# Gate rows of the mLSTM layer: three transfers inside SBUF and two VectorE additions in place of two selecting matmuls

## The chip, the cores and the metric

One core of one Trainium2 chip runs the whole program. The metric is device time in microseconds. TensorE (PE) does the matmuls, VectorE (DVE), ScalarE (ACT) and GpSimd (POOL) work beside it, SyncE (SP) issues most transfers; SBUF is the on-chip memory of 128 partitions, PSUM the matmuls' result memory of 8 banks.

## The reference, cut to what matters

The program is a trunk of two layers over 512 tokens of width 1024: layer 0 mixes tokens by an mLSTM, layer 1 by differential attention; both add a cross-attention into 256 memory tokens and a SwiGLU. The change touches the two gates of the mLSTM, eight columns of the first projection:

```python
h = rmsnorm(x, norm1[0])
p = h @ w_in
gates = p[..., 4 * MIX_WIDTH:4 * MIX_WIDTH + 2 * M_HEADS] + gate_b
i_pre, f_pre = gates[..., :M_HEADS], gates[..., M_HEADS:]
...
log_f = jax.nn.log_sigmoid(f_pre)
bc = jnp.cumsum(log_f, axis=-1)
```

Beside it stands the memory's projection, `rmsnorm(mem, mem_norm) @ w_mem_kv`, whose first tile comes right behind the changed place on PE.

## The kernel before, in words

Activations lie transposed: partitions are features, the free axis holds the 512 tokens. Every float32 product is made of three matmuls on rounded parts: a weight tile of 128 columns is split into `w_hi` (its rounding) and `w_lo` (the rest), an activation into `Hh`/`Hl` (or `Ah`/`Al`), and PE adds hi·hi, hi·lo and lo·hi over 8 chunks: 24 matmuls for a tile. POOL makes `w_hi` of a tile with one instruction (L561) and `w_lo` with four (L566); for tile n of the first projection it waits until PE is done with tile n-3 (`dense_done`), whose slot it overwrites. SP loads the raw weights ahead.

The order of the work is written out by hand in one list per engine; semaphores join them. The first projection's tiles are `PROJ`: q0, q1, v0, v1, m0, q2, m1, q3, m2, q4, m3, v2, ... (q for query and key columns, v for values, m for the memory's keys and values, 256 tokens wide). Each result leaves its PSUM bank through VectorE (`scaled_out`, `mem_out`), which divides by the norm and frees the bank.

How the gates are computed before the change:
- In the first tile, PE also multiplies by `wg`, whose columns 0 to 7 are the rounded gate weights and 8 to 15 their rests. Bank 6 then holds 16 rows: input gate, forget gate (4 heads each) by the rounded weights, and the same two groups of 4 by the rests.
- VectorE scales these 16 rows into `tmp[6]` (L1113) and raises `g_free`.
- The first half of a gate's value plus its second half is wanted on partitions 0 to 3. PE does both at once with two fp32 matmuls by the 0/1 matrix `C_GSEL` (L1628, L1629): the input gate goes to bank 6, the forget gate to bank 3. Semaphore `gsel_done`.
- ScalarE (L688 to L693) takes the forget gate from bank 3 through bias, Abs, Exp and Ln; VectorE (L1143 to L1149) forms the running sums; L1147 reads the input gate from bank 6.

The places beside it that the prediction speaks of: `mem_lo(0)` on VectorE (L1048, called after L1127) makes the low part `Al` of the memory's eight chunks with eight instructions that read `mT` and `Ah`, both in SBUF; `m_tile(0)` on PE is tile m0 and waits chunk by chunk for them (`mg_ready`); ahead of it stands the small matmul on `rm` (`mss_done`), and behind it `v_tr(0)`, four transposes. `first_tap(c)` is ScalarE's first step of the convolution, `conv(c)` VectorE's other three; `lamw` and `lame` (L1126, L1127) are two tiny VectorE instructions of the second layer's lambda. `link(...)` makes an engine wait for its own instruction before it issues the next. `dense_free` counts freed banks. `b_sq` (L876) is the second layer's place where ScalarE issues transfers inside SBUF (`QKR<-QKP`, 32 rows each), and L511 SP's transfer of the 4 rows of `Mrow` to a DRAM tensor, on which the next transfers of that queue (L515) wait.

```python
v_tile(1)
pe.wait_ge(g_free, 1)
pe.wait_ge(std_done, 1)
mm(PS[0:MH, 6], cn[0:16, C_GSEL:C_GSEL + MH], tmp[6][0:16, 0:SEQ])
mm(PS[0:MH, 3], cn[0:16, C_GSEL + MH:C_GSEL + 2 * MH], tmp[6][0:16, 0:SEQ]).then_inc(gsel_done, 1)
pe.wait_ge(msum_done, 1)
mm(PS[:, 7, 0:MEM], ones[:], rm[:]).then_inc(mss_done, 1)
m_tile(0)
v_tr(0)
q_tile(2)
```

Of the kernel before, what the change touches and what calls it, by code (L numbers as in the profile page):

```python
# [28 lines left out]
ALU = mybir.AluOpType  # L29
ACT = mybir.ActivationFunctionType  # L30
# [4 lines left out]
SEQ = 512  # L35
# [7 lines left out]
MH = 4  # L43
# [22 lines left out]
C_ID, C_BD, C_ROT, C_NEG, C_BIG, C_SEL, C_GSEL, C_INV = 0, 128, 256, 384, 512, 640, 640 + MH * P, 640 + MH * P + 8  # L66
# [52 lines left out]
def at_tile(kind, i):  # L119
    return PROJ.index((kind, i))  # L120
# [46 lines left out]
def hybrid_trunk(nc, x_t, mem_t, positions, wt, wg_cols, a_gate_b, b_lambda, prm_cols, con, out):  # L167
    ctx = ExitStack()
    with ctx:
        def sb(name, shape, dt=F32, scope=ctx):  # L170
            return scope.enter_context(nc.sbuf_tensor(name, shape, dt))

        def sem(name):
            return ctx.enter_context(nc.semaphore(name))

        PS = ctx.enter_context(nc.psum_tensor("PS", [P, 8, 512], F32))
# [10 lines left out]
        cn = sb("cn", [P, N_CON])  # L187
# [23 lines left out]
        tmp = [sb(f"tmp{i}", [P, 516]) for i in range(8)]  # L211
# [13 lines left out]
        gb = sb("gb", [MH, 2], scope=sA)  # L225
# [49 lines left out]
        g_free = sem("g_free")  # L275
# [37 lines left out]
        gsel_done = sem("gsel_done")  # L313
# [267 lines left out]
        def _(act):  # L581
            link_n = [0]

            def link(ins):
                link_n[0] += 1
                ins.then_inc(ach, 1)
                act.wait_ge(ach, link_n[0])
# [42 lines left out]
            def mem_hi(l):  # L630
                for k in range(KD):
                    nc.scalar.activation(flat(Ah[:, 4 * l:4 * l + 4])[:, k * MEM:(k + 1) * MEM],
                                         mT[:, k], ACT.Copy,
                                         scale=gcol[:, R_MN + 8 * l + k:R_MN + 8 * l + k + 1]).then_inc(mhi, 1)

            def first_tap(c):
                act.wait_ge(dense_free, at_tile("q", c) + 1)
                if c == 1:
                    act.wait_ge(mstd_done, 1)
                if c >= 2:  # L640
                    act.wait_ge(qk_ready, c - 1)
                nc.scalar.activation(PS[:, CV_BANK[c % 2]], tmp[2 + c % 2][:, 3:3 + SEQ], ACT.Identity,
                                     scale=gcol[:, R_CW + 3 * QKC + c:R_CW + 3 * QKC + c + 1],
                                     bias=gcol[:, R_CB + c:R_CB + c + 1]).then_inc(conv_first, 1)
# [34 lines left out]
            nc.scalar.activation(msq.rearrange("p n k -> p k n"), mT[:], ACT.Square).then_inc(msq_done, 1)  # L679
            mem_hi(0)  # L680
            first_tap(0)
            act.wait_ge(mss_done, 1)
            nc.scalar.activation(rm[:], PS[:, 7, 0:MEM], ACT.Sqrt, scale=1.0 / D, bias=epsc[:]).then_inc(mstd_done, 1)
            first_tap(1)
            v_out(0)

            act.wait_ge(gsel_done, 1)
            link(nc.scalar.activation(tmp[0][0:MH, 0:SEQ], PS[0:MH, 3], ACT.Identity, bias=gb[:, 1:2]))  # L688
            link(nc.scalar.activation(tmp[1][0:MH, 0:SEQ], tmp[0][0:MH, 0:SEQ], ACT.Abs))
            link(nc.scalar.activation(tmp[1][0:MH, 0:SEQ], tmp[1][0:MH, 0:SEQ], ACT.Exp, scale=-1.0))  # L690
            act.wait_ge(lam_s, 1)
# [319 lines left out]
        def _(dve):  # L1011
            link_n = [0]

            def link(ins):
                link_n[0] += 1
                ins.then_inc(vch, 1)
                dve.wait_ge(vch, link_n[0])

            def col(r):
                return gcol[:, r:r + 1]  # L1020
# [102 lines left out]
            link(nc.vector.tensor_scalar(gx[:, 4:5], col(R_BK), 8.0, None, ALU.mult))  # L1123
            nc.vector.tensor_copy(gx[:, 3:4], col(R_BQ)).then_inc(gx_ready, 1)
            dve.wait_ge(lam_in, 32)
            link(nc.vector.tensor_tensor(lamw[:], lamv[0:1, 0:4:2], lamv[0:1, 1:4:2], ALU.mult))  # L1126
            nc.vector.tensor_reduce(lame[0:1, 0:2], lamw[:], AX.X, ALU.add).then_inc(lam_s, 1)  # L1127
            mem_lo(0)
# [9 lines left out]
            b_row, a_row = tmp[5][0:MH, 0:SEQ], tmp[6][0:MH, 0:SEQ]  # L1138
# [2 lines left out]
                                           ALU.add, ALU.subtract).then_inc(lam_d, 1)  # L1141
            dve.wait_ge(lnf_done, 1)
            link(nc.vector.scalar_tensor_tensor(L, F, 0.0, L, ALU.min, ALU.subtract))  # L1143
            link(nc.vector.memset(tmp[7][0:MH, 0:SEQ], 1.0))
            dve.wait_ge(vT_done, 2)
            link(nc.vector.tensor_tensor_scan(b_row, tmp[7][0:MH, 0:SEQ], L, 0.0, ALU.mult, ALU.add))
            link(nc.vector.scalar_tensor_tensor(a_row, PS[0:MH, 6], gb[:, 0:1], b_row, ALU.add, ALU.subtract))  # L1147
            link(nc.vector.tensor_tensor_scan(Mrow[:], a_row, a_row, 0.0, ALU.max, ALU.max))
            nc.vector.tensor_tensor(tmp[0][0:MH, 0:SEQ], Mrow[:], b_row, ALU.add).then_inc(a_ready, 1)  # L1149
            mem_out(1)  # L1150
# [373 lines left out]
        def _(pe):  # L1524
            def mm(out_, a, b, start=True, stop=True):
                return nc.tensor.matmul(out_, a, b, start=start, stop=stop)  # L1526
# [98 lines left out]
            v_tile(1)  # L1625
            pe.wait_ge(g_free, 1)
            pe.wait_ge(std_done, 1)
            mm(PS[0:MH, 6], cn[0:16, C_GSEL:C_GSEL + MH], tmp[6][0:16, 0:SEQ])  # L1628
            mm(PS[0:MH, 3], cn[0:16, C_GSEL + MH:C_GSEL + 2 * MH], tmp[6][0:16, 0:SEQ]).then_inc(gsel_done, 1)  # L1629
            pe.wait_ge(msum_done, 1)  # L1630
            mm(PS[:, 7, 0:MEM], ones[:], rm[:]).then_inc(mss_done, 1)
            m_tile(0)
# [518 lines left out]
```

## Time and profile before

| what | value |
|---|---|
| median of 3 runs | 1240.56 us (1239.69 to 1241.76) |
| the profiled execution | 1240.49 us, its span 1238.7 us |
| PE busy | 1231.1 us, 99% |
| POOL busy | 840.9 us, 68% |
| DVE busy | 512.7 us, 41% |
| ACT busy | 352.1 us, 28% |
| instructions | 15969 |

Times in the rows are microseconds from the start of the span unless marked ns. A row of a timeline gives the start, the duration, engine, line, operation, result and sources, how many were merged, and in brackets how long the engine was idle before it and what ended that. An issue of a transfer has a q behind its engine's name. The time beyond the span lies around the profiled instructions.

### The profile page before, as it was taken

What the parts mean: (1) busy time and instruction counts of PE and PEld (TensorE: products, weight loads), DVE (VectorE), ACT (ScalarE), POOL (GpSimd) and SP (SyncE); (2) the same over time, 40 slices, a digit from 0 to 9 for tenths busy, and PEclk for the clock granted to TensorE, in tenths of its full rate; (3) what the DMA queues carried; (4) which work ended last, traced back from release to release, by engine and by line L of the source; (5) the groups of instructions that cost most, each with busy time, mean ns of one, the idle gap of its engine ahead of it and who ended that gap; (6) DMA issues with size and microseconds to landing.
All of it is one profiled execution on the core that took longest, in us unless ns stands there. A gap on an engine that the chain in (4) does not pass through costs nothing.

```text
span 1238.7 us, 15969 instructions
## 1 busy us (share of the span) xinstructions
PE 1231.1 (99%) x5800; PEld 1000.1 (81%) x5800; DVE 512.7 (41%) x787; ACT 352.1 (28%) x700; POOL 840.9 (68%) x1029
## 2 busy tenths in 40 slices
PE   9999999999999999999999999999999999999998
PEld 7888877788888888888887777778888888888887
DVE  6954434634322233112344777775433112221331
ACT  6523456543210011001141666645322001100110
POOL 7998333467777777777776444436687777777775
PEclk9999999999999999999999999999999999999999
DMA  7234111122332222222233222222222223222223
GB/s 271 92 120 153 68 52 40 64 86 94 102 102 89 98 102 87 100 102 98 76 132 102 70 69 69 62 77 67 89 97 101 94 94 102 97 90 102 94 73 105
DMA packets 35067, 116.99 MB, mean 94 GB/s; under 512 B 4417, under 2 KB 4930, under 8 KB 34886
## 3 DMA queue, kind: packets, MB, share of 16 engines
q1 hardware_dynamic: 33416, 112.82, 26.8%
q10 hardware_dynamic: 1598, 3.51, 1.1%
q8 instruction: 29, 0.48, 0.2%
q14 instruction: 24, 0.20, 0.1%
HBM read 111.05 MB, written 2.11 MB: 91 GB/s over the span
## 4 chain that ended last, share of the span: by engine, by line
PE 94%; DVE 2%; POOL 1%; ACT 1%; DMA 1%; SPq 0%; issue 0%; DVEq 0%; POOLq 0%; ACTq 0%
PE PS L1526 92%; DMA w_raw<-in_wt_dram 1%; POOL w_lo L566 1%; PE PS L1920 0%; DVE nmB L1432 0%; DVE PS L1031 0%; SPq L475 0%; DVE Al L1256 0%; DVE PB L1444 0%; PE PS L1765 0%; PE PS L1948 0%; DVE PB L1443 0%; PE PS L1891 0%; DVE PS L1430 0%; PE PS L1883 0%
## 5 line engine op out<-in xcount | busy, mean ns | idle before, releaser
L566 POOL TENSOR_TENSOR w_lo<-w_raw,w_hi 128x256 fp32r<-128x256 f32 (+1 forms) x800 | 613.6, 797 | 17.0
L561 POOL TENSOR_SCALAR w_hi<-w_raw 128x1024 fp32r<-128x1024 f32 (+2 forms) x204 | 214.4, 1051 | 365.3 <-PE PS L1526 365.1
L1526 PE MATMUL PS<-Hh,w_hi 128*128 128x512 f32 x1072 | 428.6, 400 | 1.0 <-POOL w_lo L550 0.6
L1526 PE MATMUL PS<-Hh,w_lo 128*128 128x512 f32 x1072 | 418.1, 390 | 0.0
L1526 PE MATMUL PS<-Hl,w_hi 128*128 128x512 f32 x1072 | 418.1, 390 | 0.0
L1526 PEld LDWEIGHTS PS<-Hh,w_hi 128*128 128x128 f32 x1072 | 201.4, 188 | 54.2 <-issue 12.9
L1526 PEld LDWEIGHTS PS<-Hh,w_lo 128*128 128x128 f32 x1072 | 201.3, 188 | 43.0
L1526 PEld LDWEIGHTS PS<-Hl,w_hi 128*128 128x128 f32 x1072 | 201.6, 188 | 39.5 <-issue 1.0
L1526 PE MATMUL PS<-Ah,w_hi 128*128 128x512 f32 (+1 forms) x544 | 208.0, 382 | 0.1
L1526 PE MATMUL PS<-Ah,w_lo 128*128 128x512 f32 (+1 forms) x544 | 205.1, 377 | 0.0
L1526 PE MATMUL PS<-Al,w_hi 128*128 128x512 f32 (+1 forms) x544 | 205.0, 377 | 0.0
L1526 PEld LDWEIGHTS PS<-Ah,w_hi 128*128 128x128 f32 x544 | 102.4, 188 | 21.9 <-issue 2.1
L1526 PEld LDWEIGHTS PS<-Ah,w_lo 128*128 128x128 f32 x544 | 102.3, 188 | 19.0
L852 ACT ACTIVATE tmp<-tmp 128x512 f32<-128x512 f32 x44 | 27.9, 635 | 315.1 <-DVE tmp L1356 315.1
L1526 PEld LDWEIGHTS PS<-Al,w_hi 128*128 128x128 f32 x544 | 102.4, 188 | 18.6 <-issue 0.5
L1358 DVE TENSOR_TENSOR tmp<-PS,rinv 128x512 f32<-128x512 f32 x44 | 30.4, 691 | 200.4 <-PE PS L1526 200.4
L854 ACT ACTIVATE Ah<-tmp 128x512 f32 x44 | 27.8, 632 | 251.7 <-DVE tmp L1361 251.7
L1356 DVE TENSOR_TENSOR tmp<-PS,rinv 128x512 f32<-128x512 f32 x44 | 30.4, 691 | 89.8 <-PE PS L1526 89.4
L1377 DVE TENSOR_TENSOR xT<-xT,PS 128x512 f32 x24 | 16.5, 687 | 105.8 <-PE PS L1526 105.8
L1319 DVE TENSOR_TENSOR xT<-xT,PS 128x512 f32<-128x512 f32 x40 | 27.4, 686 | 78.4 <-PE PS L1526 78.4
L1364 DVE TENSOR_TENSOR Al<-tmp,Ah 128x512 f32 x44 | 41.0, 931 | 40.0 <-ACT Ah L854 40.0
L1361 DVE TENSOR_TENSOR tmp<-tmp 128x512 f32<-128x512 f32 x44 | 39.4, 895 | 5.4
(256 smaller groups left out, 965.2 us busy)
## 6 DMA issues: line engine op xcount, KB each, us to landing
w_raw<-in_wt_dram SPq DMA_DIRECT2D x181, 512.0 KB, 3.2
w_raw<-in_wt_dram SPq DMA_DIRECT2D x16, 384.0 KB, 3.1
w_raw<-in_wt_dram SPq DMA_DIRECT2D x8, 448.0 KB, 3.2
QKR<-QKP ACTq DMA_DIRECT2D x24, 128.0 KB, 4.2
xT<-in_x_t_dram SPq DMA_DIRECT2D x8, 256.0 KB, 5.5
out_dram<-xT SPq DMA_DIRECT2D x8, 256.0 KB, 2.0
mT<-in_mem_t_dram SPq DMA_DIRECT2D x1, 1024.0 KB, 10.6
cn<-in_constants_dram SPq DMA_DIRECT2D x1, 580.5 KB, 8.0
```

Of the source, the lines that this page charges most:

```text
L561: nc.gpsimd.tensor_scalar(w_hi[:, sl, 0:nk], w_raw[:, raw, 0:nk], 0.0, 1.0, ALU.add, ALU.mult).then_inc(w_round, 1)
L566: lo = nc.gpsimd.tensor_tensor(w_lo[:, sl, w], w_raw[:, raw, w], w_hi[:, sl, w].bitcast(F32), ALU.subtract)
L852: nc.scalar.activation(tmp[0][:, 0:SEQ], tmp[1][:, 0:SEQ], ACT.Silu).then_inc(silu_done, 1)
L854: nc.scalar.activation(Ah[:, bass.ds(i, 1)], tmp[3][:, 0:SEQ].rearrange("p (a n) -> p a n", a=1), ACT.Copy).then_inc(f_hi, 1)
L1319: nc.vector.tensor_tensor(xT[:, k], xT[:, k], PS[:, bank], ALU.add).then_inc(dense_free, 1)
L1356: nc.vector.tensor_tensor(tmp[1][:, 0:SEQ], PS[:, base % 2], rinv[:], ALU.mult).then_inc(dense_free, 1)
L1358: nc.vector.tensor_tensor(tmp[2][:, 0:SEQ], PS[:, (base + 1) % 2], rinv[:], ALU.mult).then_inc(dense_free, 1)
L1361: nc.vector.tensor_tensor(tmp[3][:, 0:SEQ], tmp[0][:, 0:SEQ], tmp[2][:, 0:SEQ], ALU.mult).then_inc(gu_ready, 1)
L1364: nc.vector.tensor_tensor(Al[:, bass.ds(i, 1)], one, Ah[:, bass.ds(i, 1)].bitcast(F32), ALU.subtract).then_inc(f_ready, 1)
L1377: nc.vector.tensor_tensor(xk_, xk_, PS[:, b:b + 1], ALU.add).then_inc(dense_free, 1)
L1526: return nc.tensor.matmul(out_, a, b, start=start, stop=stop)
```

## The change

On ScalarE, behind `first_tap(0)`, three transfers bring rows 4 to 7, 8 to 11 and 12 to 15 of `tmp[6]` down to partitions 0 to 3 of `tmp[0]`, `tmp[7]` and `tmp[1]`. On VectorE, ahead of lamw, two additions join the halves: the forget gate in `tmp[0]`, the input gate in `tmp[6]`. The two matmuls go. ScalarE's first gate step reads SBUF instead of bank 3, and the later `a_row` instruction SBUF instead of bank 6. VectorE waits for the second addition (`g_free` at 3) before it clears `tmp[7]`.

```diff
             mem_hi(0)
             first_tap(0)
+            act.wait_ge(g_free, 1)
+            for row, dst in ((1, tmp[0]), (2, tmp[7]), (3, tmp[1])):
+                act.dma_start(dst[0:MH, 0:SEQ], tmp[6][row * MH:(row + 1) * MH, 0:SEQ]).then_inc(gsel_done, 16)
             act.wait_ge(mss_done, 1)
...
-            act.wait_ge(gsel_done, 1)
-            link(nc.scalar.activation(tmp[0][0:MH, 0:SEQ], PS[0:MH, 3], ACT.Identity, bias=gb[:, 1:2]))
+            act.wait_ge(g_free, 2)
+            link(nc.scalar.activation(tmp[0][0:MH, 0:SEQ], tmp[0][0:MH, 0:SEQ], ACT.Identity, bias=gb[:, 1:2]))
...
             dve.wait_ge(lam_in, 32)
+            dve.wait_ge(gsel_done, 48)
+            nc.vector.tensor_tensor(tmp[0][0:MH, 0:SEQ], tmp[0][0:MH, 0:SEQ], tmp[1][0:MH, 0:SEQ], ALU.add).then_inc(g_free, 1)
+            nc.vector.tensor_tensor(tmp[6][0:MH, 0:SEQ], tmp[6][0:MH, 0:SEQ], tmp[7][0:MH, 0:SEQ], ALU.add).then_inc(g_free, 1)
             link(nc.vector.tensor_tensor(lamw[:], lamv[0:1, 0:4:2], lamv[0:1, 1:4:2], ALU.mult))
             nc.vector.tensor_reduce(lame[0:1, 0:2], lamw[:], AX.X, ALU.add).then_inc(lam_s, 1)
             mem_lo(0)
...
+            dve.wait_ge(g_free, 3)
             link(nc.vector.memset(tmp[7][0:MH, 0:SEQ], 1.0))
...
-            link(nc.vector.scalar_tensor_tensor(a_row, PS[0:MH, 6], gb[:, 0:1], b_row, ALU.add, ALU.subtract))
+            link(nc.vector.scalar_tensor_tensor(a_row, a_row, gb[:, 0:1], b_row, ALU.add, ALU.subtract))
...
             v_tile(1)
             pe.wait_ge(g_free, 1)
             pe.wait_ge(std_done, 1)
-            mm(PS[0:MH, 6], cn[0:16, C_GSEL:C_GSEL + MH], tmp[6][0:16, 0:SEQ])
-            mm(PS[0:MH, 3], cn[0:16, C_GSEL + MH:C_GSEL + 2 * MH], tmp[6][0:16, 0:SEQ]).then_inc(gsel_done, 1)
             pe.wait_ge(msum_done, 1)
```

VectorE's instructions from the last gx copy to mem_lo(0) and conv(0), before:

```order
L1124 COPY gx<-gcol 128x1 [waits vch]
L1126 TENSOR_TENSOR lamw<-lamv 1x128 [waits lam_in]
L1127 TENSOR_REDUCE lame<-lamw 1x2 [waits vch]
L1048 SCALAR_TENSOR_TENSOR Al<-mT,gcol,Ah 128x256 [waits mhi] x8
L1108 SCALAR_TENSOR_TENSOR PS<-tmp,gcol,PS 128x512 [waits conv_first,dense_free]
```

and in the change:

```order
L1127 COPY gx<-gcol 128x1 [waits vch]
L1130 TENSOR_TENSOR tmp<-tmp 4x512 [waits gsel_done,lam_in]
L1131 TENSOR_TENSOR tmp<-tmp 4x512
L1132 TENSOR_TENSOR lamw<-lamv 1x128
L1133 TENSOR_REDUCE lame<-lamw 1x2 [waits vch]
L1051 SCALAR_TENSOR_TENSOR Al<-mT,gcol,Ah 128x256 [waits mhi] x8
L1111 SCALAR_TENSOR_TENSOR PS<-tmp,gcol,PS 128x512 [waits conv_first,dense_free]
```

Two additions now stand ahead of lamw, lame and the eight instructions of mem_lo(0), and the first of them waits for the transfers.

PE's instructions between the end of v_tile(1) and m_tile(0) (the matmuls on Ah), before:

```order
L1526 MATMUL PS<-Hh,w_lo 128x512
L1526 MATMUL PS<-tmp,cn 4x512 [waits std_done,g_free]
L1526 MATMUL PS<-tmp,cn 4x512
L1526 MATMUL PS<-rm,ones 128x256 [waits msum_done]
L1526 MATMUL PS<-Ah,w_hi 128x256 [waits mg_ready,dense_free,w_split]
```

and in the change:

```order
L1533 MATMUL PS<-Hh,w_lo 128x512
L1533 MATMUL PS<-rm,ones 128x256 [waits msum_done,std_done,g_free]
L1533 MATMUL PS<-Ah,w_hi 128x256 [waits mg_ready,dense_free,w_split]
```

The matmul on rm now follows v_tile(1) directly; everything behind it keeps its order.

## Rows read from the trace of the kernel before

**Rows 1.** The page: busy time of PE, and the chain that ended last by engine

```profile
PE 1231.1 (99%) x5800; PEld 1000.1 (81%) x5800; DVE 512.7 (41%) x787; ACT 352.1 (28%) x700; POOL 840.9 (68%) x1029
PE 94%; DVE 2%; POOL 1%; ACT 1%; DMA 1%; SPq 0%; issue 0%; DVEq 0%; POOLq 0%; ACTq 0%
```

**Rows 2.** Waits of PE in the whole run: us in total, times, longest

```profile
PE PS L1765 <- DVE tmp L1283: 0.9, 1, 0.9
```

**Rows 3.** Timeline of PE around the selecting matmuls

```profile
34.69 0.39 PE L1526 MATMUL PS<-Hh,w_lo 128*128 128x512 f32 x1
35.01 1.88 PE L1526 MATMUL PS<-tmp,cn 16*4 16x512 f32 x4
36.81 0.70 PE L1526 MATMUL PS<-rm,ones 128*128 128x256 f32 x2
37.16 0.47 PE L1526 MATMUL PS<-Ah,w_hi 128*128 128x256 f32 x1
...
40.22 0.60 PE L1589 MATMUL PS<-cn,tmp 128*128 128x128 f32 x4
```

**Rows 4.** Timeline of DVE in the same stretch

```profile
34.51 0.27 DVE L1126 TENSOR_TENSOR lamw<-lamv 1x128 f32<-1x128 f32 x1
34.81 0.27 DVE L1127 TENSOR_REDUCE lame<-lamw 1x2 f32<-1x128 f32 x1
35.02 3.23 DVE L1048 SCALAR_TENSOR_TENSOR Al<-mT,gcol,Ah 128x256 fp32r<-128x256 f32 x8
```

**Rows 5.** Timeline of POOL in the same stretch

```profile
35.24 3.93 POOL L561 TENSOR_SCALAR w_hi<-w_raw 128x1024 fp32r<-128x1024 f32 x1 [1.48 <-PE PS L1526]
```

**Rows 6.** Timelines at mem_lo(1): DVE, its eight together and the first alone, then POOL

```profile
57.28 7.34 DVE L1048 SCALAR_TENSOR_TENSOR Al<-mT,gcol,Ah 128x256 fp32r<-128x256 f32 x8
57.28 0.90 DVE L1048 SCALAR_TENSOR_TENSOR Al<-mT,gcol,Ah 128x256 fp32r<-128x256 f32 x1
56.86 1.05 POOL L561 TENSOR_SCALAR w_hi<-w_raw 128x1024 fp32r<-128x1024 f32 x1
57.99 3.42 POOL L566 TENSOR_TENSOR w_lo<-w_raw,w_hi 128x256 fp32r<-128x256 f32 x4
```

**Rows 7.** Timelines of DVE and POOL at the gate's running maximum

```profile
51.30 1.50 DVE L1148 TENSOR_TENSOR_SCAN Mrow<-tmp 4x512 f32<-4x512 f32 x1
52.84 1.36 DVE L1149 TENSOR_TENSOR tmp<-Mrow,tmp 4x512 f32<-4x512 f32 x1
51.70 1.96 POOL L561 TENSOR_SCALAR w_hi<-w_raw 128x1024 fp32r<-128x1024 f32 x1
```

**Rows 8.** One line's instructions: duration in ns, min/median/max

```profile
L1361 DVE TENSOR_TENSOR tmp<-tmp x44: 694/904/906, 294.3 to 1203.4; 128x512 f32<-128x512 f32 x44
```

**Rows 9.** Timeline of ACT: at the changed place, and at a transfer of layer 1

```profile
30.61 0.76 ACT L642 ACTIVATE PS<-tmp,gcol 128x512 f32<-128x512 f32 x1
37.55 0.47 ACT L683 ACTIVATE rm<-PS,epsc 128x256 f32<-128x256 f32 x1 [6.18 <-PE PS L1526]
...
684.76 0.67 ACT L911 ACTIVATE PB<-PS,nmB,rqk_all 128x384 f32<-128x384 f32 x1 [1.36 <-DVE nmB L1433]
684.83 0.51 ACTq L876 DMA_DIRECT2D QKR<-QKP  x1
```

**Rows 10.** Timeline of SP's queue; then the QKR transfers, landing by min/median/max

```profile
114.30 0.33 SPq L511 DMA_DIRECT2D m_rows<-Mrow  x1
115.73 0.80 SPq L515 DMA_DIRECT2D Ah<-m_rows  x2
...
L876 ACTq DMA_DIRECT2D QKR<-QKP x24: 514/612/687, 654.9 to 805.9; - x24
DMA to landing us min/median/max: 2.3/4.2/5.6
```

**Rows 11.** Timelines at tile q4: DVE's mem_out(1), POOL's w_lo of it, PE's start

```profile
54.12 0.41 DVE L1088 TENSOR_TENSOR kv<-PS,rm 128x256 f32<-128x256 f32 x1
53.75 3.15 POOL L566 TENSOR_TENSOR w_lo<-w_raw,w_hi 128x256 fp32r<-128x256 f32 x4
57.78 0.40 PE L1526 MATMUL PS<-Hh,w_hi 128*128 128x512 f32 x1
```

## The prediction

> **What bounds the kernel now.** I read the page's busy times and its chain that ended last first: TensorE (PE) works 1231.1 of 1238.7 us and carries 94% of the chain [rows 1]. So a microsecond counts only if it moves when PE's next matmul can start. PE's waits of the whole run come second: the longest behind VectorE is 0.9 us [rows 2], in a later stage. The third view is PE's timeline around the changed place, and there the reader is to see an unbroken line of starts [rows 3]: after the last matmul of v_tile(1) at 34.69 come the two selecting matmuls (fp32, four passes) at 35.01, the mss matmul at 36.81, m_tile(0) from 37.16, and the transposes of v_tr(0) at 40.22. I use 40.22 as the mark: PE has no wait in its list between there and the head stage beyond 180 us, so what shifts this mark shifts the end, if nobody else becomes late.
>
> The fourth view is VectorE over the same time [rows 4]: behind the last gx copy lamw 34.51, lame 34.81, and from 35.02 the eight mem_lo instructions (0.40 us apart, 3.23 in all, done at 38.25). Each step of m_tile(0) waits for its own mem_lo. PE starts at 37.16 and needs the eighth only about 39.85, so mem_lo leads by 1.6 us at its end. The fifth view is GpSimd (POOL), which shares work time with VectorE: its rounding of the tile for m1 was released at 35.24 and took 3.93 us [rows 5] where the same instruction alone takes 1.05 [rows 6]. It ended at 39.17, 0.92 us after the last mem_lo. So it stood still for as long as the stream of mem_lo ran.
>
> **The change, part by part.**
>
> *Two matmuls removed.* PE's start of the mss matmul moves from 36.81 to about 35.01: 1.80 us off PE's line [rows 3]. Its other waits (msum_done, g_free, std_done) were met long before. m_tile(0) could then start at 35.36 and, at its present 3.06 us, end at 38.42.
>
> *Three transfers added, issued by ScalarE.* They stand behind first_tap(0), which starts at 30.61. ScalarE's transfers of the second layer are issued 0.07 us after the start of the activation ahead of them [rows 9], so the first goes out at 30.7 (31.4 if it waits for the activation's end). An 8 KB transfer with 4 rows, the nearest in size, took 0.33 to issue [rows 10]; with some 0.04 between two the third goes out at 31.4 (or 32.1). ScalarE was idle until 37.55, so the issues cost nothing there; without that cover they would cost it 1.1 us. Landing has bounds only: that 8 KB transfer had landed 1.4 us after its issue, since the queue's next transfer that waits for it went out at 115.73; SBUF to SBUF transfers of 32 rows took 2.3 at least, 4.2 in the median and 5.6 at most [rows 10]. I take 2.3, the nearest in kind and still eight times as many rows: landed at 33.7 (34.4 on the later start), just ahead of VectorE's arrival at 34.5. Both ends are kept below: at 1.4 nothing changes, at 4.2 to 5.6 it is a rival.
>
> *Two additions on VectorE, between the gx copy and lamw.* Both read two SBUF tensors; 4 by 512 costs what 128 by 512 does, and the nearest, such a tensor_tensor, took 0.694 at least and 0.904 in the median [rows 8]. Pitch is about 0.07 less than duration, as in mem_lo. Uncontended: add 1 at 34.51, add 2 at 35.11 or a little later, lamw 35.72, lame 36.01, mem_lo ready at 36.22 instead of 35.02. These 1.20 us alone would take most of PE's gain: mem_lo would end at 39.45, the last step of m_tile(0) takes 0.37, and the mark comes at 39.85, 0.4 us early.
>
> *What the additions do to the port.* This is the term that decides. POOL's rounding is still released at 35.24, since v_tile(1) is untouched. Before, it fell into a stream of two-input VectorE instructions and got nothing until its end. Now the stream is add 1, add 2, lamw, and then it breaks: lame waits for a semaphore and reads one tensor alone. Such a break lets POOL in: at 51.70 POOL's rounding was released under VectorE's scan (51.30, 1.50 us), the next VectorE instruction waits for a semaphore, and POOL ended at 53.66, which is 1.05 of work from 52.61, while that VectorE instruction, started at 52.84, needed 1.36 us and ended 0.54 after POOL [rows 7]. So I expect POOL at work from about 35.9 to 36.95, and mem_lo's first, issued at 36.22, held until then. This is the situation of mem_lo(1) nearly to the tenth: rounding from 56.86 to 57.91, first mem_lo issued at 57.28 and ended at 58.18; after it VectorE and POOL take turns, and the eight take 7.34 us instead of 3.23, POOL's four subtractions 3.42, 0.88 apart [rows 6]. For mem_lo(0) that gives: first ended 36.95 + 0.27 = 37.22; four more against POOL's four subtractions, 4 x 0.88, to 40.74; then POOL has nothing, because its next tile waits for the end of m_tile(0), and the last three come at 0.40, ending at 41.9. The last step of m_tile(0) makes it 42.3. Against 40.22: **+2.1 us**, instead of the 1.8 gained.
>
> The Trainium skill (SBUF — State Buffer, "SBUF: two separate sides") says the shared port pair is an exclusive lock held for one whole instruction, by whichever of the two started first. By that rule POOL would enter after add 2 and not after lamw, and it would have entered after the first mem_lo in the run before; the trace differs there, with 3.93 us through the whole stream. The sum by the rule is some 0.2 us more, +2.3, and I keep +2.1.
>
> *Who is late next.* VectorE comes out of mem_lo 3.65 us later than before. Behind it are conv(0), v_raw(1), the reciprocal of rm, mem_out(0), conv(1) and q_out(2), which had to wait for PE by nearly a microsecond and now doesn't. mem_out(1), which frees the bank for q4, started at 54.12 and q4 at 57.78 [rows 11]; it moves by about 3, q4 by 2.1, so 2.3 us of slack stay. POOL had tile q4 ready at 56.90, 0.9 us ahead of PE [rows 11], the smallest lead I found; its earlier tile waits on PE and moves with it, the a_row operation that now has two SBUF inputs can cost it up to 0.7. So nothing more lands on PE; without that lead it would be up to 0.7. The ScalarE chain of the gates starts after v_out(0) as before and moves with PE. The clear of tmp and the wait on g_free ahead of it are long met: 0. The a_row operation itself: 0.74 before from PSUM [the same place as rows 7], 0.7 to 1.4 now, inside the slack.
>
> **Sum.** Profiled execution: 1240.49 us (span 1238.7). Removed -1.80, given back and more by mem_lo's lateness +3.9: net +2.1, 1242.6. The profiled execution lies 0.07 below the median 1240.56, so the two starting points are the same here.
>
> **Rivals.**
> 1. *POOL doesn't get in.* If the break at lame is too short, or POOL stays locked out as at 35.24, mem_lo runs at 0.40 and the mark comes at 39.85 to 39.9: -0.3 to -0.4, 1240.1. For it: 3.93 us of standing still in [rows 5]. Against it: [rows 7], and a break here that is longer, as lame runs in it.
> 2. *The transfers land late* (the slower side). The point from which it decides is 35.24: landing between 34.5 and there adds its lateness one to one; landing later, POOL's rounding runs first (to 36.3), and the additions too take turns with POOL. Landing 4.2 after issue, at 35.65: add 1 ends at 36.85, add 2 about 37.9, lame 38.8, mem_lo from then against POOL's last two subtractions to 40.1, six more at 0.40: 42.5, mark 42.9, +2.7. Landing 5.6 after, at 37.0: mark about 43.6, +3.4. So 1243.2 to 1243.9. For it: the median of the 24 transfers [rows 10]. Against it: 4 rows instead of 32, and 1.4 us measured for the nearest size.
> 3. *The gain is kept.* If m_tile(0) were not held by mem_lo at all, -1.8, 1238.7. Against it: mem_lo can't end before 39.45 and PE wants its eighth at 38.05. Only if a later wait of PE had swallowed the lateness could this appear, and there is none of that size.
>
> **How the numbers follow.** Forecast 0.61, rival 1 0.14, rival 2 0.18, rival 3 0.03, the rest (a later tile of POOL's late, up to +0.7 on top) 0.04. About 0.2%, 2.5 us, is what a measurement of this kernel can tell from no change, so slower begins above 1243.0. The forecast lies 0.4 below that: with runs that spread from 1239.69 to 1241.76 I give a quarter of it to slower (0.15), with most of rival 2 (0.16) and of the rest (0.02): 0.33. Faster: part of rival 3 and scatter, 0.03. Same: 0.64. The range: from rival 1 less some scatter, 1239.8, to rival 2's later landing plus scatter, 1244.4. The forecast's own range is 1242.0 to 1243.3.
>
> **What would show it.** In the changed profile: the mss matmul at about 35.0 (matmuls really off the line); three small transfers issued from ScalarE at 30.7 to 32.1; VectorE's first addition at 34.5 with no idle row behind a transfer (else rival 2); POOL's w_hi released at 35.24 ending near 37, not 40 (else rival 1); mem_lo(0) as eight in some 5.7 us, ended at 41.9; the first transpose of v_tr(0) at 42.3, and a PE wait behind VectorE's Al of some microseconds that was not there. The prediction is wrong if the mark stands at 40 or earlier, or if the mark is at 42.3 and the end is not 2 us later.

## The result, and the profile after

| | before | with the change |
|---|---|---|
| median | 1240.27 us (1239.67 to 1241.76, 11 runs) | 1244.62 us (1242.27 to 1246.05, 11 runs) |
| profiled execution, its span | 1240.49, 1238.7 | 1245.39, 1242.8 |
| PE busy | 1231.1 | 1232.9 |
| VectorE busy | 512.7 | 517.6 |
| mean granted clock of the runs | 1.0 in nearly all | 0.997 to 0.999 |

The ratio is 1.0033, with a 95% interval of 1.0025 to 1.0041: 4.35 us slower. That is twice the forecast +2.1, past the 1243.0 from which the prediction called it slower, and 0.2 us above its range's upper end. I read the changed profile in the same order as before. The busy times and the chain by engine, on its profile page:

```profile
PE 1232.9 (99%) x5796; PEld 1001.8 (81%) x5796; DVE 517.6 (42%) x789; ACT 352.1 (28%) x700; POOL 840.1 (68%) x1029
PE 93%; DVE 4%; POOL 1%; ACT 1%; DMA 1%; issue 1%; SPq 0%; DVEq 0%; ACTq 0%; POOLq 0%
```

VectorE's share of the chain went from 2% [rows 1] to 4%. The waits of PE in the whole run (total, times, longest) name the place; the first of these two stood nowhere before, the second is [rows 2] under its new line number:

```profile
PE PS L1533 <- DVE Al L1051: 2.6, 2, 2.4
...
PE PS L1770 <- DVE tmp L1290: 0.9, 1, 0.9
```

PE's timeline at the changed place, against [rows 3]; the program's opening ended 0.40 earlier in this execution, so its times stand 0.40 lower for that alone:

```profile
34.29 0.39 PE L1533 MATMUL PS<-Hh,w_lo 128*128 128x512 f32 x1
34.52 0.59 PE L1533 MATMUL PS<-rm,ones 128*128 128x256 f32 x2
37.54 0.36 PE L1533 MATMUL PS<-Ah,w_hi 128*128 128x256 f32 x1 [2.43 <-DVE Al L1051]
...
38.31 0.39 PE L1533 MATMUL PS<-Ah,w_hi 128*128 128x256 f32 x1 [0.19 <-DVE Al L1051]
...
41.28 0.41 PE L1533 MATMUL PS<-Ah,w_lo 128*128 128x256 f32 x1
...
42.82 0.60 PE L1596 MATMUL PS<-cn,tmp 128*128 128x128 f32 x4
```

The rm matmul follows v_tile(1) at once. Then PE idles 2.43 us for mem_lo's first result (such an idle time with its releaser in brackets I call a listed wait), and the mark, the first transpose of v_tr(0), stands at 42.82. I call D the time from the last matmul of v_tile(1) to the mark: 5.53 before (34.69 to 40.22), 8.53 now.

VectorE and POOL in the same stretch, for [rows 4] and [rows 5]:

```profile
34.11 0.68 DVE L1130 TENSOR_TENSOR tmp<-tmp 4x512 f32<-4x512 f32 x1
34.72 0.67 DVE L1131 TENSOR_TENSOR tmp<-tmp 4x512 f32<-4x512 f32 x1
35.32 1.11 DVE L1132 TENSOR_TENSOR lamw<-lamv 1x128 f32<-1x128 f32 x1
36.46 0.27 DVE L1133 TENSOR_REDUCE lame<-lamw 1x2 f32<-1x128 f32 x1
36.67 4.91 DVE L1051 SCALAR_TENSOR_TENSOR Al<-mT,gcol,Ah 128x256 fp32r<-128x256 f32 x8
```

```profile
34.84 1.46 POOL L561 TENSOR_SCALAR w_hi<-w_raw 128x1024 fp32r<-128x1024 f32 x1 [1.46 <-PE PS L1533]
36.38 3.33 POOL L566 TENSOR_TENSOR w_lo<-w_raw,w_hi 128x256 fp32r<-128x256 f32 x4
```

The additions start with no idle time behind a transfer. POOL's rounding ends at 36.30, so its 1.05 us of work began at 35.25, with lamw held up under it (1.11 instead of 0.27). mem_lo(0) takes 4.91 us and ends at 41.58. The transfers, on ScalarE's queue:

```profile
27.85 0.73 ACTq L684 DMA_DIRECT2D tmp<-tmp  x1
...
28.61 0.59 ACTq L684 DMA_DIRECT2D tmp<-tmp  x1
...
29.24 0.58 ACTq L684 DMA_DIRECT2D tmp<-tmp  x1
```

What I had not priced is in the table by stretches (busy time and count of PE, PEld, DVE, ACT, POOL; then granted clock, DMA share, GB/s); first two stretches of after in m_tile(0), then one in layer 1, and the same work of layer 1 before:

```profile
38.00:40.00 2.00, 1.71 (x8) 1.18 (x6) 2.00 (x4) 0.00 (x0) 1.71 (x2) 0.66 0.00 0
40.00:42.00 2.00, 2.00 (x10) 1.95 (x10) 2.00 (x5) 0.00 (x0) 0.00 (x0) 0.50 0.64 227
...
696.00:700.00 4.00, 4.00 (x21) 3.48 (x20) 4.00 (x5) 1.96 (x3) 2.26 (x3) 0.68 0.17 35
```

```profile
693.00:697.00 4.00, 4.00 (x26) 3.52 (x26) 4.00 (x6) 1.83 (x3) 2.75 (x4) 1.00 0.09 16
```

After its idle time PE's granted clock fell to half, 1.2 of 2.4 GHz: the 256-column matmuls start 0.21 apart (41.07, 41.28, 41.49) instead of 0.12. It fell again at 696. The books of the two profiled executions: start -0.40, D +3.00, from the mark to the end +1.55 (1200.02 against 1198.47, nearly all in that second stretch), outside the span +0.75 (2.55 against 1.80). Together 4.90, the difference of 1245.39 and 1240.49. The step of 1.5 us lies in that one stretch: the same ScalarE instruction stood 2.5 us later than before at 684.76, and 4.1 later at 699.74.

### The profile page after: what moved, and what is told of

Read it like the earlier page. It is cut to its first block, busy times and chain, and to the rows that moved or that the text cites. A ratio compares the mean times of both kernels' runs of the same rounds, so it can differ in the third digit from the quotient of the medians.

```text
span 1242.8 us, 15968 instructions
## 1 busy us (share of the span) xinstructions
PE 1232.9 (99%) x5796; PEld 1001.8 (81%) x5796; DVE 517.6 (42%) x789; ACT 352.1 (28%) x700; POOL 840.1 (68%) x1029
## 4 chain that ended last, share of the span: by engine, by line
PE 93%; DVE 4%; POOL 1%; ACT 1%; DMA 1%; issue 1%; SPq 0%; DVEq 0%; ACTq 0%; POOLq 0%
PE PS L1533 91%; POOL w_lo L566 1%; DMA w_raw<-in_wt_dram 1%; PE PS L1925 0%; DVE nmB L1439 0%; DVE PS L1034 0%; DVE Al L1263 0%; SPq L475 0%; DVE PB L1451 0%; PE PS L1770 0%; PE PS L1953 0%; DVE rinv L1075 0%; PE PS L1896 0%; DVE PB L1450 0%; DVE PS L1437 0%
```

## The experiments

Twelve runs follow, each timed 5 to 11 times, in three groups (1 to 4, 5 to 8, 9 to 12), each group beside the kernel before on the same chip (its medians 1240.07, 1240.22 and 1239.93). My theory: the additions make mem_lo(0) late and let POOL into its stream, which starves PE and costs it its clock. Rivals: the transfers, the removed matmuls or a later wait cost it.

**1. The additions behind mem_lo(0).**

```diff
-            dve.wait_ge(gsel_done, 48)
-            nc.vector.tensor_tensor(tmp[0][0:MH, 0:SEQ], tmp[0][0:MH, 0:SEQ], tmp[1][0:MH, 0:SEQ], ALU.add).then_inc(g_free, 1)
-            nc.vector.tensor_tensor(tmp[6][0:MH, 0:SEQ], tmp[6][0:MH, 0:SEQ], tmp[7][0:MH, 0:SEQ], ALU.add).then_inc(g_free, 1)
             link(nc.vector.tensor_tensor(lamw[:], lamv[0:1, 0:4:2], lamv[0:1, 1:4:2], ALU.mult))
             nc.vector.tensor_reduce(lame[0:1, 0:2], lamw[:], AX.X, ALU.add).then_inc(lam_s, 1)
             mem_lo(0)
+            dve.wait_ge(gsel_done, 48)
+            nc.vector.tensor_tensor(tmp[0][0:MH, 0:SEQ], tmp[0][0:MH, 0:SEQ], tmp[1][0:MH, 0:SEQ], ALU.add).then_inc(g_free, 1)
+            nc.vector.tensor_tensor(tmp[6][0:MH, 0:SEQ], tmp[6][0:MH, 0:SEQ], tmp[7][0:MH, 0:SEQ], ALU.add).then_inc(g_free, 1)
             conv(0)
```

> The change, with its two additions (and their wait for the transfers) moved behind the eight mem_lo(0) instructions. I measure D, from the start of the last matmul of v_tile(1) to the first transpose of v_tr(0): 5.53 us before, 8.53 with the change. Theory (the additions make mem_lo late, which lets GpSimd into its stream, which starves PE and drops its clock): mem_lo(0) starts 1.2 us earlier than in the sum of the prediction and runs 0.40 apart, so PE is held by its last one only: D about 3.9, no stretch at half clock, time 1.6 us below the kernel before (ratio 0.9987). Rival (the cost lies in the transfers or in what reads the gates later): D may shrink, but the time stays above that of before.

Measured: 1241.25, ratio 1.0010 (1.0001 to 1.0019). D 4.09 (34.03 to 38.12), clock 1.0 in all runs: the first half holds. The second doesn't. From VectorE, POOL and the waits of PE:

```profile
34.36 3.24 DVE L1051 SCALAR_TENSOR_TENSOR Al<-mT,gcol,Ah 128x256 fp32r<-128x256 f32 x8
37.53 1.52 DVE L1133 TENSOR_TENSOR tmp<-tmp 4x512 f32<-4x512 f32 x1
38.98 1.22 DVE L1134 TENSOR_TENSOR tmp<-tmp 4x512 f32<-4x512 f32 x1
```

```profile
34.58 3.94 POOL L561 TENSOR_SCALAR w_hi<-w_raw 128x1024 fp32r<-128x1024 f32 x1 [1.47 <-PE PS L1533]
38.60 3.59 POOL L566 TENSOR_TENSOR w_lo<-w_raw,w_hi 128x256 fp32r<-128x256 f32 x4
```

```profile
PE PS L1533 <- POOL w_lo L566: 1.5, 2, 1.2
```

POOL stands still through mem_lo(0) as before (3.94) and now also takes turns with the additions (3.59 for its four subtractions instead of 2.83). PE, 1.44 us earlier relative to v_tile(1), waits 1.5 us for weights at q4 and v2, and from the mark to the end it takes 1200.40 instead of 1198.47. The median outside the span is 2.53, 0.7 above before. So D -1.44, behind the mark +1.93 and outside the span +0.7 make the 1.2 us by which this run is slower, where 1.6 faster was expected. Of any time that PE gains here, POOL's lead at q4, which the prediction gave as 0.9 us [rows 11], lets through no more than that, and less where POOL is slower itself.

**2. The additions alone,** in the kernel before: two of the same shape on unused rows of tmp[7], ahead of lamw; matmuls kept, no transfers.

```diff
             dve.wait_ge(lam_in, 32)
+            nc.vector.tensor_tensor(tmp[7][0:MH, 0:SEQ], tmp[7][0:MH, 0:SEQ], tmp[7][0:MH, 0:SEQ], ALU.add).then_inc(g_free, 1)
+            nc.vector.tensor_tensor(tmp[7][32:32 + MH, 0:SEQ], tmp[7][32:32 + MH, 0:SEQ], tmp[7][32:32 + MH, 0:SEQ], ALU.add).then_inc(g_free, 1)
...
+            dve.wait_ge(g_free, 3)
             link(nc.vector.memset(tmp[7][0:MH, 0:SEQ], 1.0))
```

> The kernel before with its selecting matmuls, no transfers, and two additions of the same shape (results unused) ahead of lamw. Theory: mem_lo(0) becomes as late as with the change, GpSimd's w_hi takes about 1.5 us instead of 3.9, and the mark comes 2.1 to 2.3 us later than before: D 7.6 to 7.9. PE's idle time is shorter by the 1.8 us of the matmuls, so if a long idle stretch is what drops the clock, no half-clock stretch here; time 2.1 to 2.3 us above before (ratio 1.0018). If instead the wait steps alone drop it, D 8.5 and ratio above 1.0025. Rival (removed matmuls or transfers cause the loss): D 5.5 to 6.7, time within 1 us of before.

Measured: 1242.92, ratio 1.0023 (1.0013 to 1.0033). POOL's w_hi 1.57, and VectorE:

```profile
35.38 1.01 DVE L1128 TENSOR_TENSOR lamw<-lamv 1x128 f32<-1x128 f32 x1
36.42 0.27 DVE L1129 TENSOR_REDUCE lame<-lamw 1x2 f32<-1x128 f32 x1
36.62 4.91 DVE L1048 SCALAR_TENSOR_TENSOR Al<-mT,gcol,Ah 128x256 fp32r<-128x256 f32 x8
```

The same 4.91 us as with the change. D is 8.25 (34.13 to 42.38), between the two values expected, and the clock did fall, though PE's listed wait was only 0.5 us:

```profile
38.00:40.00 2.00, 2.00 (x8) 1.44 (x7) 2.00 (x4) 0.34 (x1) 1.67 (x2) 0.50 0.00 0
```

So the additions by themselves make the stretch; transfers and removed matmuls aren't needed, and a long single wait isn't needed for the half clock. The time is 2.85 above before.

**3. The port kept clear:** POOL's rounding of tile m1 (n is 6) waits until all eight instructions of mem_lo(0) are done.

```diff
+                if n == 6:
+                    pool.wait_ge(mg_ready, 8)
                 nc.gpsimd.tensor_scalar(w_hi[:, sl, 0:nk], w_raw[:, raw, 0:nk], 0.0, 1.0, ALU.add,
```

> The change, with GpSimd's rounding of the tile for m1 held back until all eight mem_lo(0) are done. Theory (GpSimd's turns stretch mem_lo): lamw 0.3 us, mem_lo(0) 3.2 us instead of 4.9, D about 5.1 to 5.2, time 0.4 us below before (ratio 0.9997) if the clock holds. Rival (mem_lo is late for the additions alone, the port matters little): D stays above 7.

Measured: 1242.05, ratio 1.0013 (1.0004 to 1.0022); D 5.33 (34.35 to 39.68), clock 1.0. With the port to itself VectorE shows the prediction's uncontended case:

```profile
35.41 0.27 DVE L1134 TENSOR_TENSOR lamw<-lamv 1x128 f32<-1x128 f32 x1
35.72 0.27 DVE L1135 TENSOR_REDUCE lame<-lamw 1x2 f32<-1x128 f32 x1
35.92 3.23 DVE L1053 SCALAR_TENSOR_TENSOR Al<-mT,gcol,Ah 128x256 fp32r<-128x256 f32 x8
```

```profile
PE PS L1535 <- DVE Al L1053: 1.4, 1, 1.4
PE PS L1535 <- POOL w_lo L568: 1.3, 2, 1.0
```

3.2 of D's 8.53 us are thus owed to POOL's turns and what follows from them. The time is 2.0 us above before, where 0.4 below was expected: the weights held back are late at q4 and v2 by 1.3 us, and the median outside the span is 2.70, 0.9 above before.

**4. PE's idle time filled.**

```diff
             mm(PS[:, 7, 0:MEM], ones[:], rm[:]).then_inc(mss_done, 1)
-            m_tile(0)
+            def fill(count):
+                for _ in range(count):
+                    mm(PS[:, 3], Hh[:, 0, 0:P], Hh[:, 0])
+            fill(9)
+            m_tile(0, after=lambda k: fill(1) if k < 5 else None)
```

> The change, with 9 idle-time matmuls of 128x512 into bank 3 ahead of m_tile(0) and one more after each of its first five steps (results unused). Theory (0.9 us of the loss is the clock that falls to half after PE's idle stretch, and the rest is mem_lo's lateness): granted clock 1.0 throughout this stretch, D about 7.7 instead of 8.5, time 2.1 to 2.3 us above before (ratio 1.0018). Rival (the half clock costs nothing, as PE only waits for VectorE): D stays 8.5 whatever the clock.

Measured: 1243.13, ratio 1.0024 (1.0015 to 1.0034). Clock 1.0 in all ten runs, but D 8.17 (34.68 to 42.85): here the fillers between the steps got in the way, PE was 0.8 us behind the last mem_lo. It settles nothing on the price of the clock; run 10 repeats it without them.

**5. The removal alone,** in the kernel before: the two matmuls go and nothing takes their place. The forget gate and the input gate are both computed from the first four rows, so the halves made by the rests and the forget gate's own rows are left out.

```diff
-            act.wait_ge(gsel_done, 1)
-            link(nc.scalar.activation(tmp[0][0:MH, 0:SEQ], PS[0:MH, 3], ACT.Identity, bias=gb[:, 1:2]))
+            act.wait_ge(g_free, 1)
+            link(nc.scalar.activation(tmp[0][0:MH, 0:SEQ], tmp[6][0:MH, 0:SEQ], ACT.Identity, bias=gb[:, 1:2]))
...
-            link(nc.vector.scalar_tensor_tensor(a_row, PS[0:MH, 6], gb[:, 0:1], b_row, ALU.add, ALU.subtract))
+            link(nc.vector.scalar_tensor_tensor(a_row, a_row, gb[:, 0:1], b_row, ALU.add, ALU.subtract))
...
-            mm(PS[0:MH, 6], cn[0:16, C_GSEL:C_GSEL + MH], tmp[6][0:16, 0:SEQ])
-            mm(PS[0:MH, 3], cn[0:16, C_GSEL + MH:C_GSEL + 2 * MH], tmp[6][0:16, 0:SEQ]).then_inc(gsel_done, 1)
```

> The two selecting matmuls are gone and nothing takes their place: no transfers, no additions; the gates are computed from the first four rows alone, so half of the gates' values and the forget gate's own rows are left out. It asks what the removal is worth by itself. By PE's line alone D falls from 5.53 to about 3.8 to 3.9 and the time by 1.6 us (1238.6, ratio 0.9987). By GpSimd's lead (tile q4 was ready 0.9 us ahead of PE, v2 1.0) PE stands still at q4 and v2 and keeps 0.9 us at most: time 0.7 to 0.9 us below before, ratio 0.9993. I expect the second.

Measured: 1240.19, ratio 1.0000 (0.9991 to 1.0009). D 4.08 (34.98 to 39.06), then 0.7 us of waits for weights, 1199.08 from the mark to the end: inside the span 0.8 us are left of the 1.8 that went. And outside it there are 2.56 us in the median instead of 1.80, which takes that too. So even with nothing in its place the removal gave no gain that can be told from none; the 0.7 to 0.9 us expected came inside the span only.

```profile
PE PS L1526 <- POOL w_lo L566: 0.7, 2, 0.3
```

**6. The transfers alone,** in the kernel before, into unused rows of tmp[7].

```diff
             first_tap(0)
+            act.wait_ge(g_free, 1)
+            for row, dst in ((1, tmp[7]), (2, tmp[7]), (3, tmp[7])):
+                act.dma_start(dst[row * 32:row * 32 + MH, 0:SEQ], tmp[6][row * MH:(row + 1) * MH, 0:SEQ]).then_inc(extra, 16)
...
+            dve.wait_ge(extra, 48)
             link(nc.vector.scalar_tensor_tensor(a_row, PS[0:MH, 6], gb[:, 0:1], b_row, ALU.add, ALU.subtract))
```

> The kernel before with the three transfers of the change on ScalarE's queue (into unused rows), matmuls kept, no additions. In the runs so far the kernels with transfers have 2.5 to 2.7 us between the span and the run's time (median), those without 1.8. If the transfers cause that, the span stays within 0.3 us of before (D 5.5) and the time outside the span rises by 0.7: ratio 1.0006. If it comes from something else in the change, both stay: ratio 1.0000.

Measured: 1240.23, ratio 1.0001 (0.9992 to 1.0010); D 5.53, 1.81 us outside the span in the median. The transfers cost nothing that can be seen, and my guess that they cause the time outside the span is wrong.

**7. The small work behind mem_lo(0) too,** and **8. its control.** Run 7 is run 1 with the gx, lamw and lame instructions moved as well, behind the additions; run 8 moves these alone, in the kernel before:

```diff
-            link(nc.vector.tensor_tensor(gx[:, 0:2], gcol[:, R_XQ:R_XQ + 2], gcol[:, R_XK:R_XK + 2], ALU.mult))
-            nc.vector.tensor_scalar(gx[:, 2:3], col(R_SL), 1.0 - LAMBDA_INIT, None, ALU.mult)
-            link(nc.vector.tensor_scalar(gx[:, 4:5], col(R_BK), 8.0, None, ALU.mult))
-            nc.vector.tensor_copy(gx[:, 3:4], col(R_BQ)).then_inc(gx_ready, 1)
             dve.wait_ge(lam_in, 32)
-            link(nc.vector.tensor_tensor(lamw[:], lamv[0:1, 0:4:2], lamv[0:1, 1:4:2], ALU.mult))
-            nc.vector.tensor_reduce(lame[0:1, 0:2], lamw[:], AX.X, ALU.add).then_inc(lam_s, 1)
             mem_lo(0)
+            link(nc.vector.tensor_tensor(gx[:, 0:2], gcol[:, R_XQ:R_XQ + 2], gcol[:, R_XK:R_XK + 2], ALU.mult))
+            nc.vector.tensor_scalar(gx[:, 2:3], col(R_SL), 1.0 - LAMBDA_INIT, None, ALU.mult)
+            link(nc.vector.tensor_scalar(gx[:, 4:5], col(R_BK), 8.0, None, ALU.mult))
+            nc.vector.tensor_copy(gx[:, 3:4], col(R_BQ)).then_inc(gx_ready, 1)
+            link(nc.vector.tensor_tensor(lamw[:], lamv[0:1, 0:4:2], lamv[0:1, 1:4:2], ALU.mult))
+            nc.vector.tensor_reduce(lame[0:1, 0:2], lamw[:], AX.X, ALU.add).then_inc(lam_s, 1)
             conv(0)
```

> The change, with its additions and also the gx and lamw/lame instructions moved behind mem_lo(0). mem_lo(0) then starts a microsecond earlier, ahead of GpSimd's rounding, and ends a microsecond earlier, so GpSimd stands still for about 1.9 instead of 2.9 us: D 3.7 to 3.8, PE's wait at q4 and v2 down from 1.5 to 0.5 to 0.9 us, span 0.8 to 1.0 us below before. With 0.7 us outside the span for the transfers the time is 0 to 0.3 us below before, ratio 0.9998 to 1.0000. If GpSimd's lead isn't the limit, it gives no more than the additions' move alone (ratio 1.001).

> The kernel before with the gx and lamw/lame instructions moved behind mem_lo(0), and nothing else: the control for the run above. PE sets the end and waits for nobody here, so D stays 5.53 and the time within 0.3 us of before; only GpSimd's lead at q4 grows, by up to a microsecond.

Measured: run 7 1244.14, ratio 1.0032 (1.0020 to 1.0044); run 8 1240.36, ratio 1.0002 (0.9993 to 1.0011), D 5.53. Run 7 is a clear miss: D is 5.28 (33.76 to 39.04), not 3.7 to 3.8. mem_lo(0) did start earlier, and POOL's rounding, released at 34.31, got in and took turns from there:

```profile
33.06 5.46 DVE L1051 SCALAR_TENSOR_TENSOR Al<-mT,gcol,Ah 128x256 fp32r<-128x256 f32 x8
38.45 1.21 DVE L1127 TENSOR_TENSOR tmp<-tmp 4x512 f32<-4x512 f32 x1
39.59 1.52 DVE L1128 TENSOR_TENSOR tmp<-tmp 4x512 f32<-4x512 f32 x1
```

```profile
PE PS L1533 <- DVE kv L1091: 2.4, 2, 1.2
...
PE PS L1596 <- DVE tmp L1086: 0.9, 1, 0.9
```

With everything behind it late, VectorE itself became the bound: PE waited at v_tr(1) and for the banks of q4 and v2, 1202.28 us from the mark to the end. The 2.3 us of slack that the prediction gave VectorE at q4 were used up.

The control, run 8, shows the same turns with no addition and no transfer in the kernel:

```profile
34.21 5.46 DVE L1048 SCALAR_TENSOR_TENSOR Al<-mT,gcol,Ah 128x256 fp32r<-128x256 f32 x8
35.43 1.34 POOL L561 TENSOR_SCALAR w_hi<-w_raw 128x1024 fp32r<-128x1024 f32 x1 [1.47 <-PE PS L1526]
```

PE didn't wait for it, since mem_lo(0) had started 1.0 us earlier against v_tile(1) and the selecting matmuls still stood ahead of m_tile(0). POOL's lead at q4 shrank to 0.6 us (ready at 57.34, q4 at 57.97), where it was expected to grow.

**9. The additions last,** directly ahead of mem_lo(0), with lamw and lame ahead of them.

```diff
+            link(nc.vector.tensor_tensor(lamw[:], lamv[0:1, 0:4:2], lamv[0:1, 1:4:2], ALU.mult))
+            nc.vector.tensor_reduce(lame[0:1, 0:2], lamw[:], AX.X, ALU.add).then_inc(lam_s, 1)
             dve.wait_ge(gsel_done, 48)
             nc.vector.tensor_tensor(tmp[0][0:MH, 0:SEQ], tmp[0][0:MH, 0:SEQ], tmp[1][0:MH, 0:SEQ], ALU.add).then_inc(g_free, 1)
             nc.vector.tensor_tensor(tmp[6][0:MH, 0:SEQ], tmp[6][0:MH, 0:SEQ], tmp[7][0:MH, 0:SEQ], ALU.add).then_inc(g_free, 1)
-            link(nc.vector.tensor_tensor(lamw[:], lamv[0:1, 0:4:2], lamv[0:1, 1:4:2], ALU.mult))
-            nc.vector.tensor_reduce(lame[0:1, 0:2], lamw[:], AX.X, ALU.add).then_inc(lam_s, 1)
             mem_lo(0)
```

> The change with lamw and lame ahead of its two additions, which now stand directly ahead of mem_lo(0), so no instruction that waits or that reads one SBUF tensor alone lies in VectorE's stream when GpSimd asks for the port. If GpSimd gets in only at a break of the stream (as the prediction had it), it stands still until mem_lo(0) ends as in the kernel before (w_hi near 4.8 us), mem_lo(0) takes 3.2 us, D is 5.2 to 5.3, no half clock, and the time 1.0 to 2.0 us above before (q4 and v2 then wait for GpSimd; ratio 1.0012). If it gets in behind a single instruction of the additions (as it did in the change, under lamw), w_hi takes about 1.5 us, mem_lo(0) 4.9 us, D 8.3 to 8.5 and the time is that of the change.

Measured: 1242.68, ratio 1.0019 (1.0010 to 1.0028), D 6.13 (33.88 to 40.01): neither of the two. The time is 2.75 above before. VectorE and POOL:

```profile
34.20 0.67 DVE L1132 TENSOR_TENSOR tmp<-tmp 4x512 f32<-4x512 f32 x1
34.80 1.53 DVE L1133 TENSOR_TENSOR tmp<-tmp 4x512 f32<-4x512 f32 x1
36.25 3.24 DVE L1051 SCALAR_TENSOR_TENSOR Al<-mT,gcol,Ah 128x256 fp32r<-128x256 f32 x8
```

```profile
34.43 1.35 POOL L561 TENSOR_SCALAR w_hi<-w_raw 128x1024 fp32r<-128x1024 f32 x1 [1.49 <-PE PS L1533]
35.87 6.30 POOL L566 TENSOR_TENSOR w_lo<-w_raw,w_hi 128x256 fp32r<-128x256 f32 x4
```

POOL got in right behind the first addition, with no wait between the two: a break of the stream isn't needed. But its first subtraction then stood still through the whole of mem_lo(0), 3.5 us. This profile is one at full clock throughout. Against run 10 below, also at full clock, D is 1.7 us less (6.13 against 7.86), and mem_lo's eight instructions are 1.7 shorter (3.24 against 4.93): of the 2.3 us of lateness in the change, 1.7 come of turns within mem_lo. Seven of the eleven runs show a mean clock of 0.998 or 0.999 and stand at 1242.5 to 1243.6; the four at 1.0 at 1241.1 to 1241.5. So in this one kernel runs whose clock fell are 1 to 2 us longer; where in them it fell no profile shows.

**10. Filled ahead of m_tile(0) only:** run 4 with the nine matmuls and none between the steps.

> The change with 9 idle-time matmuls ahead of m_tile(0) and none between its steps, so that nothing delays a step. If PE's idle 2.4 us ahead of m_tile(0) is what lowers the clock: clock 1.0, PE 0.4 us behind the last mem_lo, D 7.7, time 2.4 to 3.0 us above before. If the gaps between the steps lower it as well (as with the additions alone, where PE idled 0.5 us and the clock fell): half clock again and D 8.1 to 8.4.

Measured: 1242.73, ratio 1.0023 (1.0014 to 1.0032), D 7.86 (34.15 to 42.01). mem_lo(0) is as long as with the change, and the clock holds though PE was idle a third of the second stretch:

```profile
36.57 4.93 DVE L1051 SCALAR_TENSOR_TENSOR Al<-mT,gcol,Ah 128x256 fp32r<-128x256 f32 x8
```

```profile
38.00:40.00 2.00, 1.32 (x8) 0.86 (x7) 2.00 (x4) 0.00 (x0) 1.63 (x2) 1.00 0.00 0
```

So D splits: mem_lo's lateness 2.33 (7.86 less 5.53), the clock in m_tile(0) 0.67 (8.53 less 7.86). The distance from mem_lo's end to the mark says the same: 0.51 here (41.50 to 42.01), 1.24 with the change (41.58 to 42.82).

**11. Two tiny matmuls kept,** 2 columns each, results unused, where the selecting matmuls stood.

```diff
+            mm(PS[0:MH, 3, 0:2], cn[0:16, C_GSEL:C_GSEL + MH], cn[0:16, 0:2])
+            mm(PS[0:MH, 3, 0:2], cn[0:16, C_GSEL + MH:C_GSEL + 2 * MH], cn[0:16, 0:2])
             mm(PS[:, 7, 0:MEM], ones[:], rm[:]).then_inc(mss_done, 1)
```

> The change with two fp32 matmuls of 2 columns (result unused) where the selecting matmuls stood: PE issues as many instructions as before. The kernels without the selecting matmuls show 2.1 to 2.7 us between span and time in the median, those with them 1.8, whatever else they do. If the number or place of PE's instructions sets that, it goes back to 1.8 and the time is 0.7 us below the change's; if it is something else, 2.5. Inside the span nothing changes: D 8.5.

Measured: 1243.55, ratio 1.0026 (1.0016 to 1.0037). Outside the span 1.75 to 1.84 us in all eight runs: back to the value of before. Inside it D was 9.12 (34.11 to 43.23), with half clock until the end of the tile:

```profile
42.00:44.00 2.00, 2.00 (x12) 2.00 (x11) 1.93 (x4) 0.00 (x0) 0.40 (x1) 0.50 0.10 39
```

**12. The change again.**

> The change once more, as the reference on the same chip for the three above: D 8.5, time 4.3 us above before (ratio 1.0035), 2.5 us outside the span, mean clock 0.997 to 0.999. If a second stretch at half clock in layer 1 appears again at the same matmuls, it belongs to this change; if not, it is chance.

Measured: 1244.59 in five runs, ratio 1.0035 (1.0021 to 1.0048); D 8.41 (33.94 to 42.35), from the mark to the end 1198.34 and no second stretch at half clock, so that one doesn't come in every execution. 2.73 us outside the span in the median. Run 10, beside it on the same chip, is 1.86 us faster in the median: 0.9 of that lies outside the span (1.83 against 2.73) and the other 1.0 inside, where the two kernels differ by the fillers and the clock alone.

No version beat the kernel before.

## Why the prediction was right and wrong

**Removed matmuls, 1.80 us off PE's line.** Right for the start of the rm matmul (0.23 behind v_tile(1) instead of 2.12). That a gain there would be worth 1.8 to the end, had mem_lo not held it, is refuted by run 5: 0.8 inside the span, nothing in the time. Rival 3, at -1.8, didn't come true in any run.

**Transfers: early enough.** Right, and more so than I had: they went out from 27.85, not 30.7. ScalarE's queue took them up as soon as g_free allowed (VectorE's instruction that raises it ran from 27.14 to 27.81), between two of the activations that stand ahead of them in its list. I had placed them behind first_tap(0) by its start. The issue took 0.58 to 0.73 us each, not the 0.33 of [rows 10]; in run 6, with the same issue times, the kernel lost nothing. Rival 2 falls.

**Additions and port: the turns and the size are right, the point of entry isn't.** mem_lo's end relative to v_tile(1) was put at 7.2 us (34.69 to 41.9) and measured 7.29 (34.29 to 41.58). Runs 1, 2 and 3 confirm the parts: without additions ahead of it, 3.24 us of mem_lo and D 4.09; with them alone, 4.91 and 8.25; with the port clear, 3.23 and 5.33. But POOL entered behind the second addition, at 35.25, and not in the break at lame. So the hold of 0.8 us fell on lamw and not on mem_lo's first: set against the start of the kernel before, mem_lo began at 37.07 instead of 36.22 and took 4.91 instead of 5.7 us. The two differences are one wait in another place, which is why the end still came out right. The Trainium skill (SBUF — State Buffer, "SBUF: two separate sides") has the shared port pair held for one whole instruction while the other engine blocks; the entry behind the second addition agrees with it. By that rule the prediction's sum was +2.3, and run 10 measured 2.33. The eight instructions of mem_lo in the kernel before and in run 9 don't agree with it: there POOL waited through them all, its instruction lengthened to 3.93 us from 1.05 and to 4.22 from 0.74. Rival 1 falls, as the port did open.

**"Who is late next: nothing more lands on PE" is the step that failed.** It looked at VectorE and POOL and never at PE's own clock. The sum let PE stand idle ahead of m_tile(0) and between its steps, and put the mark 0.4 us behind mem_lo's end, at the pace of [rows 3] (24 matmuls in 3.06 us). The granted clock fell to half instead, and the mark came 1.24 behind it. Against run 10's D that is 0.67 us in the profiled execution, 0.55 in run 12 and 1.3 in run 11; and in one execution another 1.5 us went in layer 1. The sum has no such term, nor is there a rival for it; these figures would have made one of +0.5 to +2 on top.

**And the 1.8 us between span and time was taken as fixed.** It rose to 2.5 in the median, and run 11 shows that this belongs to the removed matmuls, not how. Together: 2.3 by lateness, 0.7 outside the span, which leaves 1.3 of the median's 4.35. That is a remainder and not a measurement; the clock accounts for most of it, by the 1.0 us between runs 10 and 12. That the time came close to the range's upper end owes nothing to rival 2, for which that end was set: the transfers were early.

POOL's lead at q4, named as the smallest, proved a limit in runs 1, 3 and 5 (0.7 to 1.5 us of waits there), though in the change itself PE was too late to need it.

## What to carry to other kernels

Work that is small on VectorE can be dear by where it stands: two additions of together 1.3 us ahead of a stream that another engine consumes step by step, and that takes turns with POOL, made PE 2.3 us late although 1.8 us had been taken off it, and its clock fell as well. When a forecast gives the bounding engine a new wait, it should carry the clock's price with it; and before pricing work removed from that engine, look up how far its suppliers are ahead: here a lead of 0.9 us let 0.8 through of 1.4.

## What the runs showed of the hardware that was not expected

- **Port turns differ with the moment.** In four kernels (before, runs 1, 5 and 6) the rounding was released 0.22 or 0.23 us after the start of the first of mem_lo's eight and waited for all of them, 3.92 to 3.94 us long. In runs 7 and 8 it was released 0.06 and 0.04 after the start of the fourth (34.31 and 35.43) and got in; behind an addition it got in each time. Where it had got in, the two engines mostly alternated from there, but not in run 9, where the next POOL instruction was locked out again. Moment within an instruction and place in the stream weren't varied apart, so what decides it stays open.
- **The length of the listed waits doesn't tell when the clock falls.** In the profiles it fell in run 2 with one of 0.5 us, and held in run 10 with 1.1 us in four pieces, in run 3 with 1.4 and in run 9 with 2.2 us. The mean clock was below 1.0 in all 16 runs of the change, in seven of eleven in run 9 and in eight of nine in run 2; but also, at 0.999, in 2 of the 82 timings of the kernel before beside the experiments.
- **Time outside the span.** Kernels with the selecting matmuls, or with other matmuls near their place, show 1.8 us in the median (runs 2, 6, 8, 10, 11), with single timings up to 2.8; run 4 shows 2.06. Those without show 2.2 to 2.7, with single timings from 1.8 to 3.1. Two matmuls of 2 columns brought it back. What takes this time the profile doesn't show.
- **Transfers overtake.** ScalarE's queue issued the first of them at 27.85, while six of the activations that precede it in the program's order had not started. In run 6 the order was the same (28.72, under the first activations of mem_hi(0)).
